# Attention on expanded values: heads written feature-major by two column halves, reciprocals turned and spread per block

## What is computed

```python
q_abs = jnp.einsum('blhd,hcd->blhc', q, w_uk) * (ATT_HEAD_DIM ** -0.5)
...
sc = jnp.einsum('bqhc,bqkc->bqhk', qa.astype(jnp.float32), c_sel.astype(jnp.float32))
sc = jnp.where(valid[:, :, None, :], sc, -jnp.inf)
p = jax.nn.softmax(sc, axis=-1).astype(c.dtype)
o_lat = jnp.einsum('bqhk,bqkc->bqhc', p, c_sel)
return jnp.einsum('bqhc,hcd->bqhd', o_lat, w_uv)
```

## Time and profile before

| | us |
|---|---|
| median of 3 runs | 4052.51 |
| lowest and highest | 4051.61, 4058.08 |
| the profiled execution | 4047.39 |
| its span, first to last instruction | 4045.6 |
| mean granted TensorE clock in it | 0.955 |

### The profile page before, as it was taken

The page is one execution under the profiler, slowest core; times in us unless marked ns, Lnnn a source line. Parts: engine busy times, 40 slices in busy tenths (PEclk is TensorE's granted clock), DMA queues, the critical chain, the costliest instruction groups (busy, mean ns, idle before and its releaser), DMA issues. The chain is left out here.

```text
span 4045.6 us, 67444 instructions
## 1 busy us (share of the span) xinstructions
PE 3552.8 (88%) x30260; PEld 2864.1 (71%) x30260; DVE 1902.7 (47%) x2754; ACT 1153.2 (29%) x1730; POOL 75.8 (2%) x85
## 2 busy tenths in 40 slices
PE   1999799999757777779999999999778899999998
PEld 0888677887246667747888888667556668888885
DVE  6565446652666655455222222557684452222226
ACT  2211222222533333333111111245364331111113
POOL 0000000000000000000000000020000020000000
PEclk8999899999779999979999999999899999999999
DMA  4223311231732221142111111211000211111112
GB/s 174 92 103 108 126 65 42 76 104 71 262 113 61 76 76 40 46 153 72 49 51 47 47 52 45 75 40 37 6 1 1 72 49 51 47 47 52 47 44 92
DMA packets 142836, 284.68 MB, mean 70 GB/s; under 512 B 8164, under 2 KB 82276, under 8 KB 142292
## 3 DMA queue, kind: packets, MB, share of 16 engines
q1 hardware_dynamic: 127252, 250.80, 19.1%
q10 hardware_dynamic: 15296, 29.57, 2.1%
HBM read 234.42 MB, written 45.65 MB: 69 GB/s over the span
## 5 line engine op out<-in xcount | busy, mean ns | idle before, releaser
L308 DVE TENSOR_TENSOR ring_b_wl<-ring_b_raw,ring_b_wh 128x1024 fp32r<-128x1024 f32 (+1 forms) x200 | 236.2, 1181 | 1137.9 <-ACT ring_b_wh L305 1137.8
L340 PE MATMUL PS<-ffn_x_high,ring_b_wh 128*128 128x512 f32 x1408 | 550.8, 391 | 7.7 <-DVE ffn_x_low L559 4.2
L341 PE MATMUL PS<-ffn_x_low,ring_b_wh 128*128 128x512 f32 x1408 | 549.9, 391 | 0.0
L342 PE MATMUL PS<-ffn_x_high,ring_b_wl 128*128 128x512 f32 x1408 | 549.8, 390 | 0.0
L305 ACT ACTIVATE ring_b_wh<-ring_b_raw 128x1024 fp32r<-128x1024 f32 (+1 forms) x200 | 204.6, 1025 | 1209.8 <-PE PS L342 1199.6
L340 PEld LDWEIGHTS PS<-ffn_x_high,ring_b_wh 128*128 128x128 f32 x1408 | 265.4, 188 | 65.4 <-DVE ffn_x_low L559 5.4
L342 PEld LDWEIGHTS PS<-ffn_x_high,ring_b_wl 128*128 128x128 f32 x1408 | 265.3, 188 | 55.2
L341 PEld LDWEIGHTS PS<-ffn_x_low,ring_b_wh 128*128 128x128 f32 x1408 | 265.3, 188 | 55.2 <-issue 0.2
L340 PE MATMUL PS<-ffn_hid_high,ring_b_wh 128*128 128x512 f32 x704 | 276.2, 392 | 2.6 <-DVE ring_b_wl L308 2.6
L342 PE MATMUL PS<-ffn_hid_high,ring_b_wl 128*128 128x512 f32 x704 | 274.2, 390 | 0.0
L341 PE MATMUL PS<-ffn_hid_low,ring_b_wh 128*128 128x512 f32 x704 | 274.2, 390 | 0.0
(11 more groups left out here) (408 smaller groups left out, 6314.6 us busy)
## 6 DMA issues: line engine op xcount, KB each, us to landing
ring_b_raw<-in_ffn_up SPq DMA_DIRECT2D x88, 512.0 KB, 3.4
norm_e_t<-in_ada SPq DMA_DIRECT2D x32, 512.0 KB, 4.1
ring_a_raw<-in_in_o SPq DMA_DIRECT2D x32, 512.0 KB, 4.2
ring_b_raw<-in_ffn_down SPq DMA_DIRECT2D x32, 512.0 KB, 3.5
scan_tin<-scan_in SPq DMA_DIRECT2D x9, 1536.0 KB, 10.0
scan_in<-um SPq DMA_DIRECT2D x20, 641.0 KB, 10.1
ring_a_raw<-in_in_e SPq DMA_DIRECT2D x24, 512.0 KB, 3.6
ring_b_raw<-in_ffn_down SPq DMA_DIRECT2D x32, 384.0 KB, 3.1
```

The source lines that it names most:

```text
L308: return nc.vector.tensor_tensor(out, x, high.bitcast(fp32), ALU.subtract)
L340: nc.tensor.matmul(out, wh, xh, start=k == 0, stop=False)
L341: nc.tensor.matmul(out, wh, xl, start=False, stop=False)
L342: last = nc.tensor.matmul(out, wl, xh, start=False, stop=k == kt - 1)
```

## The change

Instead of summing latents and multiplying by w_uv afterwards, the kernel now expands the values first. In the opening `values(k)` multiplies 128 tokens of latents with w_uv for all heads at once (eight products of 512 columns), and VectorE copies each from bank 4 or 5 to `vt`. `value(p)` then multiplies, per key block and head, 64 value features (the weights) with 128 columns of turned probabilities; the two heads of a pair write partitions 0 to 63 and 64 to 127 of bank 6 or 7, by block. The heads so stand features by tokens, and no transposes of the output are needed. Since the sums of the rows are now needed along the columns, the reciprocals (VectorE, step 1 of the next block) are turned by one small transpose (piece `turned`, step 2), copied to `rT` (8 by 128), and spread over the feature partitions by four products with the constant `heads_out` (piece `spread`, step 3); VectorE multiplies at step 5 and writes `mT`. The exp is written in place in `sm`. A fourth DMA brings `heads_out`. `lat`, `osb`, `pr`, `ctok` and their copies and semaphores are gone.

```diff
+                vt = sb(mixer, "at_values", [P, NQ, DB])
...
+                uv = xT[:, 2:4, SEQ:T]
+                spread = xT[:, 6:8, SEQ:T]
...
+                INVERT_AT, TURN_AT, SPREAD_AT, RESCALE_AT = 1, 2, 3, 5
...
-                    if n % NH == 5 and n > NH:
-                        out_at[n // NH - 1] = len(pieces)
-                        pieces.append(("out", n // NH - 1, 0))
+                    for what, at in (("turned", TURN_AT), ("spread", SPREAD_AT)):
+                        if n % NH == at and n > NH:
+                            pieces.append((what, n // NH - 1, 0))
...
+                        sp.dma_start(uv, A["w_uv"].rearrange("p (k h) d -> p k (h d)", k=2)).then_inc(S["a_loaded"], 16)
+                        sp.dma_start(xT[0:NH, 4:6, SEQ:T], A["heads_out"].rearrange("h (k j) t -> h k (j t)", k=2))\
+                            .then_inc(S["a_loaded"], 16)
...
+                        def values(k):
+                            if k >= 2:
+                                pe.wait_ge(S["a_values_ready"], k - 1)
+                            nc.tensor.matmul(bank(4 + k % 2), cT[:, k * P:k * P + P], uv, start=True, stop=True)\
+                                .then_inc(S["a_values"], 1)
+
+                        def value(p):
+                            b, j = 2 * p // NH, p % (NH // 2)
                             pe.wait_ge(S["a_turned"], upto[2 * p + 1])
-                            if p >= 2:
...
+                            if j == 0 and b >= 2:
+                                pe.wait_ge(S["a_rescaled"], b - 1)
                             for k in range(b + 1):
-                                last = nc.tensor.matmul(bank(6, 2 * P, p % 2 * 2 * P), ctok[:, k, :],
-                                                        pT[:, p % 2, k].rearrange("p h t -> p (h t)"), start=k == 0,
...
-                        for k in range(NQ):
-                            last = nc.tensor.transpose(bank(4 + k // 4, P, k % 4 * P), cT[:, k * P:k * P + P], ident[:, :])
-                        last.then_inc(S["a_ctok"], 1)
-                        pe.wait_ge(S["a_loaded"], 48)
+                                for i in range(2):
+                                    last = nc.tensor.matmul(bank(6 + b % 2, P, j * P)[64 * i:64 * i + 64],
+                                                            vt[:, k, (2 * j + i) * 64:(2 * j + i) * 64 + 64],
+                                                            pT[:, p % 2, k, i, :], start=k == 0, stop=k == b,
+                                                            skip_group_check=True)
+                                    if k == b:
+                                        last.then_inc(S["a_value"], 1)
+
+                        def spread_inverse(b):
+                            t = place["spread", b, 0]
+                            pe.wait_ge(S["a_turned"], max(t - 1, place["turned", b, 0] + 1))
+                            for j in range(NH // 2):
+                                last = nc.tensor.matmul(bank(4 + t % 2, P, j * P), heads_out(j), rT[:, :], start=True, stop=True)
+                            last.then_inc(S["a_transposed"], 1)
...
+                        pe.wait_ge(S["a_loaded"], 64)
                         for h in range(NH):
+                            values(h)
...
+                            if n % NH == TURN_AT and b >= 0:
+                                t = place["turned", b, 0]
+                                pe.wait_ge(S["a_inverse"], b + 1)
+                                pe.wait_ge(S["a_turned"], t - 1)
+                                nc.tensor.transpose(bank(4 + t % 2, P)[0:NH], rs[:, b % 2, :], ident[:, :])\
+                                    .then_inc(S["a_transposed"], 1)
+                            if n % NH == SPREAD_AT and b >= 0:
+                                spread_inverse(b)
                             if n % 2 == 0 and 0 <= n // 2 - 1 < PAIRS:
-                                latent(n // 2 - 1)
-                            if n % 2 == 1 and 0 <= (n - 3) // 2 < PAIRS:
-                                value((n - 3) // 2)
-                            if n % NH == 5 and n > NH:
-                                b = n // NH - 1
-                                pe.wait_ge(S["a_rescaled"], b + 1)
-                                turn(out_at[b], lambda k: osb[:, b % 2, k * P:k * P + P], 4)
+                                value(n // 2 - 1)
...
+                                nc.scalar.activation(sm[:, s, 0:w], sm[:, s, 0:w], ACT.Exp, bias=nmx[:, s:s + 1],
...
+                            if (n - 1) % NH == TURN_AT and o >= 0:
+                                t = place["turned", o, 0]
                                 act.wait_ge(S["a_transposed"], t + 1)
-                                nc.scalar.activation(mT[:, 0:4, o * P:o * P + P],
-                                                     bank(4 + t % 2).rearrange("p (k t) -> p k t", k=4), ACT.Copy)\
+                                nc.scalar.activation(rT[:, :], bank(4 + t % 2, P)[0:NH], ACT.Copy).then_inc(S["a_turned"], 1)
...
+                                act.wait_ge(S["a_transposed"], t + 1)
+                                if o:
+                                    act.wait_ge(S["a_rescaled"], o)
+                                nc.scalar.activation(spread, bank(4 + t % 2).rearrange("p (k t) -> p k t", k=2), ACT.Copy)\
...
+                            dve.wait_ge(S["a_exp"], NH * b + NH)
+                            nc.vector.reciprocal(rs[:, b % 2, :], rs[:, b % 2, :]).then_inc(S["a_inverse"], 1)
...
-                            dve.wait_ge(S["a_exp"], NH * b + NH)
-                            dve.wait_ge(S["a_value"], NH // 2 * (b + 1))
...
+                            dve.wait_ge(S["a_value"], NH * (b + 1))
+                            dve.wait_ge(S["a_turned"], place["spread", b, 0] + 1)
+                            out = mT[:, 0:4, b * P:b * P + P].rearrange("p (k a) t -> p k a t", k=2)
+                            nc.vector.tensor_tensor(out, bank(6 + b % 2).rearrange("p (k a t) -> p k a t", k=2, a=2),
+                                                    spread.rearrange("p k (a t) -> p k a t", a=2), ALU.mult)\
...
-                        dve.wait_ge(S["a_ctok"], 1)
-                        nc.vector.tensor_copy(ctok[:, :, :].rearrange("p k c -> p (k c)"), PS[:, 4 * 512:6 * 512])\
-                            .then_inc(S["a_ctok_ready"], 1)
+                        for k in range(NQ):
+                            dve.wait_ge(S["a_values"], k + 1)
+                            nc.vector.tensor_copy(vt[:, k], bank(4 + k % 2)).then_inc(S["a_values_ready"], 1)
...
-                            if n % NH == 2 and n > NH:
+                            if n % NH == INVERT_AT and n > NH:
+                                invert(b - 1)
+                            if n % NH == RESCALE_AT and n > NH:
```

More of the change, by code:

```diff
@@ L2855, in mixer_stage @@
                 rs = sb(mixer, "at_rs", [P, 2, NH])
-                lat = sb(mixer, "at_lat", [P, 2, 2, P])
-                osb = sb(mixer, "att_rescaled_o", [P, 2, DB])
+                rT = sb(mixer, "at_rT", [NH, P])
                 N = NQ * NH
                 PAIRS = N // 2
-                STEPS = N + 7
-                pieces, upto, out_at = [], {}, {}
+                STEPS = N + 6
+                INVERT_AT, TURN_AT, SPREAD_AT, RESCALE_AT = 1, 2, 3, 5
+                pieces, upto = [], {}
                 for n in range(STEPS):
@@ L2909, in turn @@
                             last.then_inc(S["a_transposed"], 1)
-                        def latent(p):
-                            b = 2 * p // NH
+                        def values(k):
[5 more added lines that the diff above has]
+                            b, j = 2 * p // NH, p % (NH // 2)
@@ L2920, in latent @@
-                            last.then_inc(S["a_latent"], 1)
-                        def value(p):
-                            b = 2 * p // NH
-                            pe.wait_ge(S["a_latcopy"], p + 1)
-                            if 2 * p % NH == 0 and b:
-                                pe.wait_ge(S["a_rescaled"], b)
-                            for i in range(2):
-                                h = (2 * p + i) % NH
-                                last = nc.tensor.matmul(bank(7, 64, h * 64), lat[:, p % 2, i, :], uv[:, h, :], start=True,
-                                                        stop=True)
-                            last.then_inc(S["a_value"], 1)
@@ L2996, in _ @@
                                 turned(n - 1)
[L2997 to L2999 removed]
+                            o = (n - 1) // NH - 1
+                            if (n - 1) % NH == TURN_AT and o >= 0:
+                                t = place["turned", o, 0]
                                 act.wait_ge(S["a_transposed"], t + 1)
[L3001 to L3010 removed]
+                                nc.scalar.activation(rT[:, :], bank(4 + t % 2, P)[0:NH], ACT.Copy).then_inc(S["a_turned"], 1)
```

(7 more changed lines are left out.)

43 lines of the change are left out of this document (11 added, 32 removed).

## The result

| | before | after |
|---|---|---|
| median of the runs made together, us | 4052.06 | 4087.99 |
| lowest and highest | 4049.60, 4058.08 | 4086.54, 4094.97 |
| the profiled execution, and its span | 4047.39, 4045.6 | 4094.97, 4093.1 |
| mean granted clock in it | 0.955 | 0.942 |
| attention block, in the profiled execution | 271.4 | 310.4 |

The ratio is 1.0089, with a 95% interval of 1.0072 to 1.0107. The kernel became slower, as forecast, but by 36 us instead of 13: 6 us above the range. The profiled execution of after is its slowest and lies 47.6 us above that of before. 39.0 of them lie in the attention block; 4.4 lie ahead of it and 4.2 behind, where the code is the same.

The account below looks back on a forecast made before the run. VectorE's ranking and selection set the pace to 3060.6 us, then TensorE and the score loop. Terms 13.5 - 1 + 5.2 - 3.1 - 1.6 = +13.0 us on 4047.39 gave 4060.4, median 4066, range 4055 to 4082.

Parts of the forecast that it names:

- with a denser TensorE I take 5 us at half clock: Opening: TensorE at half clock for 5 us, losing 2.5, within an opening term of +13.5 us.
- the rival on the clock: Wide blocks: each of seven new stops costs 3 to 4 us at half clock, up to +12 us; chance 0.2.
- The loss of overlap: Opening: `values` between two heads ends the overlap of paired q_abs heads; 2.58 us per head at full clock.
- The dose behind the copies: Opening: VectorE's fixed dose of key selection, 8.3 us, comes after its eight copies; first add +13.6 us.
- The second rival: Opening: most of the dose hides beside the last products or in VectorE waits, 8 us less, 4057.5; chance 0.12.
- Blocks 1 to 3: Attention blocks 1 to 3: cheaper value products against the reciprocals' spread, net -1 us, between -4 and +3.
- The stops: Blocks 4 to 7: TensorE waits at `turned` and `spread` for ScalarE's copy of the piece two before; 4.75 to 5.2 us per block.
- The first rival: Blocks 4 to 7: the new stops cost nothing; total -7 us, about 4045.5; chance 0.1.
- block 5: Attention block 5: new stops 5.2 us, less 2.2 for the old stop and 2.9 saved, +0.1 us.
- The fourth rival: Wide blocks: the granted clock falls to half at the new stops, up to +12 us, 4072 to 4078; chance 0.2.
- The savings: Cheaper value products, 0.16 us per key block and pair of heads; old `out` stop gone, 2.2 per block; tail -1.6.
- The third rival: Value products: column halves run one after the other, 0.43 us per key block; +14 us, 4080; chance 0.1.

Follow-up runs that it names:

- e5: The changed kernel with 36 needless transposes on TensorE during the wait for the block's first DMAs; 4081.32 us, ratio 1.0061 to the kernel before.
- e1: The changed kernel with all eight values products in a row ahead of q_abs; 4067.05 us, ratio 1.0028 to the kernel before.
- e10: The changed kernel with q_abs of all heads first and the values products last; one run, attention block +21.4 us against the kernel before.
- e4: The changed kernel with a seventh of VectorE's selection dose behind each of the first seven copies; one run, attention block +38.8 us against the kernel before.
- e3: The changed kernel with pieces `turned` and `spread` placed ahead of their step's head; 4068.98 us, ratio 1.0032 to the kernel before.
- e9: The changed kernel with the opening in pairs, two values products then q_abs of two heads; one run, attention block +15.6 us against the kernel before.
- e14: e13 with the two heads of a pair multiplied one after the other, not by turns; 4048.24 us, ratio 0.9996 to the kernel before.
- e13: The changed kernel with the edits of e1 and e3 together; 4041.32 us, ratio 0.9974 to the kernel before.
- e6: e3 with only the first values product left in the opening, the other seven inside steps 5 to 29; 4031.41 us, ratio 0.9950 to the kernel before.
- e2: The kernel before with q_abs heads ordered 0 2 4 6 1 3 5 7; one run, 5.2 us more to the first add, 4.7 in the block.

## Why the prediction was wrong, and where it was right

- **The failed step: "with a denser TensorE I take 5 us at half clock".** It was 45.8 us. The order at the full clock gives +14.0 (e5), the half clock the other 19.6. No bound of the term (10.5 to 15.5) held it, and the rival on the clock spoke only of the stops. It is 20.2 of the 26.0 us by which the block's sum was off. The rise of the clock was read from the mix of before, with paired heads, and carried to another mix, in which it did not come. That the order is what kept it away is shown: the same 48 records in the orders of e1 and e10 raised it about 4 us after the first. What in the mix keeps it away, the lone heads or the short groups, is open.
- *The loss of overlap* was right: `values` between two heads ends it. A head costs 2.97 us at the full clock (e5), not 2.58; seven times 0.39 ahead of the last copy is 2.7, most of why e5 shows 14.0 where the sum had 11.0 without its half clock. The 0.39 lie where 128 and 64 rows take turns: in e5's trace records of one group start 0.43 us apart, as the prediction has it, but four of the six of a round 0.52 to 0.53 ahead of the next, at those changes: 0.2 us per change. Whether the change of rows or the waits at the same places make it is not shown. The fourth DMA, put at 0.6, moved the first product from 4.47 us after the block's start to 4.56 in after, 5.10 in e1 and 5.24 in e10.
- *The dose behind the copies* stood where the forecast had it, and costs 7.4 us between e10 and e1. In after, where q_abs ran so late, it is only 3.1 (e4). The second rival, that the opening hides, falls.
- *Blocks 1 to 3*: -3.3 against -1, in its bounds of -4 to +3; the other orders of the change gave -5.1 to +1.4.
- *The stops* are real, at the named places, with VectorE idle 4.52 and 2.83 us. The first rival falls: without them (e3) blocks 4 to 7 run 5.7, 11.1, 4.9 and 5.2 us shorter than in after. The forecast's 5.2, 5.2, 4.75 and 4.75 fit blocks 4, 6 and 7 of after. **The second mis-sized term is block 5**: 11.1 (44.7 against 33.5 us) for 5.2. There `turned` waited 5.18 us, since ScalarE's copy stands behind an exp, and that behind an `add` which VectorE reached only after its selection. TensorE was busy for 1.48 of the 8.00 us from 3094 to 3102, and from 3102 to 3106 the clock is 0.50:

```profile
3104.00 0.37 PE L2969 MATMUL PS<-ident,at_rs 128*8 128x128 f32 x1 [5.18 <-ACT at_pT L2989]
3104.30 2.83 PE L2930 MATMUL PS<-at_pT,at_values 128*64 128x128 f32 x24
3107.06 2.75 PE L2906 MATMUL PS<-at_cT,at_qabs 128*128 128x512 f32 x4
```

- *The fourth rival* was right in kind and inside its bound: all stops together cost 26.8 us for a forecast of 5.2 + 5.2 + 9.5 = 19.9, so 6.9 of its "up to +12". Of the 26.8, 8.3 are records that ran slower. How much a block pays changes with the same stops: block 4 took 41.1 us in after and 43.4 to 43.9 in e1, e4, e5, e9 and e10, block 5 44.7 in after and 40.7 to 40.9 in e1, e5 and e9. No run shows why.
- *The savings* were right. Without stops blocks 5, 6 and 7 gained 5.3, 5.4 and 5.9 us (e3); the forecast implies 5.1, 6.7 and 6.0. 32 value records go by in 1.90 us (forecast 2.2), a pair of steps in block 7 in 8.24 (8.3), the tail -2.5 (-1.6). The third rival, halves in turn, falls by e14.

So the change had a sound core. Its loss came from two things beside it: where the eight products stand in the opening, and where two small pieces stand in their steps. e13 and e6 undo only these.

## What to carry to other kernels

Ask of every new order on TensorE which clock it starts at and whether it leaves parts of the array empty (e2): 100% busy is no promise of the full clock, and the rise seen in one mix can't be carried to another. Put work of a new kind where the engine already has slack (e6) rather than between two operations that overlap. When buffers go in rotation, number a small piece ahead of the wide one of the same step if its inputs are ready, since behind it, it waits for that step's slowest engine, and everything queued waits with it.

## What the runs showed of the hardware

- A mix of one 128-row, 512-column product and two of 64 rows, without a pause, kept 1.2 GHz for 45.8 us; entered at 2.4 GHz, it kept that for all its 24 us (e5).
- The rise to 2.4 GHz came 4.0 us after the first product with 128-row products in a row (e1), 3.9 and 8.4 with 64-row heads in pairs (e10, before), 15.0 with the heads of one half in a row (e2).
- Two heads on the two row halves took 2.16 us for 8 records at the full clock, one head 1.98 for 4. The 2.90 of the earlier trace rows at that clock was not TensorE's own price: heads there wait for ScalarE's copies, while in e9 the `values` stand between.
- Two column halves by turns took 0.06 us per record of 128 columns, one half at a time 0.10, with 128 rows in both.
